# Order of TensorE's small products in the mixer head output: four full products, key transposes, then the 64-column products

## The reference, cut to what matters

```python
    scores = jnp.einsum('bhncd,bhnsd->bhncs', q_dec, k_inv)
    o_intra = jnp.einsum('bhncs,bhnse->bhnce', jnp.where(mask, scores, 0.0), vc)
    kv = jnp.einsum('bhnsd,bhnse->bhnde', k_end, vc)
    ...
    s_final, s_prev = lax.scan(step, s0.astype(f32), ...)
    o_inter = jnp.einsum('bhncd,bhnde->bhnce', q_dec, s_prev)
    o = (o_intra + o_inter).reshape(B, H, T, dv)
```

## Time and profile before

| | before |
|---|---|
| median of 3 runs | 1314.87 us |
| the profiled execution's span | 1315.8 us |
| PE busy | 97% of the span |
| PE weight loads (PEld) busy | 90% |
| DVE, ACT, POOL busy | 68%, 44%, 8% |
| mean granted TensorE clock | 0.990 |

### The profile page before, as it was taken

How to read it: one execution, slowest core, us unless ns; L and a number is a source line. 1 busy time by engine, 2 the same in 40 slices (tenths; PEclk the granted TensorE clock), 3 DMA queues, 4 the chain that set the end, 5 groups by cost and what they waited for, 6 DMA issues and landing times.

```text
span 1315.8 us, 24155 instructions
## 1 busy us (share of the span) xinstructions
PE 1277.5 (97%) x10293; PEld 1188.5 (90%) x10293; DVE 900.2 (68%) x1413; ACT 581.1 (44%) x908; POOL 110.0 (8%) x161
## 2 busy tenths in 40 slices
PE   6999999999999999999999999999999999999997
PEld 3899999999998778899998998998999898899997
DVE  4577755576464564678687786786888976767567
ACT  4533355644774444535413213223165664535431
POOL 0111111000001111000000001110000110000000
PEclk8999999999999999999999999999999999999999
DMA  9997896545244453222554456675435003555550
GB/s 354 382 317 238 264 250 168 144 151 182 75 160 157 165 172 133 88 91 80 175 158 148 144 177 192 188 239 161 133 100 194 29 1 102 188 160 193 183 170 33
DMA packets 170152, 218.39 MB, mean 166 GB/s; under 512 B 6158, under 2 KB 147861, under 8 KB 169910
## 3 DMA queue, kind: packets, MB, share of 16 engines
q1 hardware_dynamic: 140196, 148.11, 34.5%
q0 software_dynamic: 29152, 67.42, 17.0%
q10 hardware_dynamic: 698, 1.32, 0.3%
HBM read 215.70 MB, written 1.12 MB: 165 GB/s over the span
## 4 chain that ended last, share of the span: by engine, by line
PE 84%; DVE 8%; ACT 3%; issue 2%; DMA 2%; SPq 1%; POOL 0%; DVEq 0%; ACTq 0%
PE bank L1356 30%; PE bank L705 12%; PE bank L724 9%; PE bank L757 7%; PE bank L740 4%; DVE wlo L2154 2%; PE bank L1260 2%; PE bank L815 1%; PE bank L1334 1%; PE bank L906 1%; PE bank L1019 1%; PE bank L1434 1%; PE bank L1502 1%; DMA graw_b<-in_w_mod 1%; PE bank L1451 1%
## 5 line engine op out<-in xcount | busy, mean ns | idle before, releaser
L2154 DVE TENSOR_TENSOR wlo<-raw,whi 128x2048 fp32r<-128x2048 f32 x131 | 297.3, 2274 | 88.9 <-ACT whi L1545 88.5
L1545 ACT ACTIVATE whi<-raw 128x2048 fp32r<-128x2048 f32 x131 | 247.9, 1898 | 183.9 <-PE bank L1356 131.2
L1356 PE MATMUL bank<-a_lo,whi 128*128 128x256 f32 (+1 forms) x688 | 165.9, 312 | 0.0
L1356 PE MATMUL bank<-whi,m_hi 128*128 128x256 f32 x576 | 161.3, 280 | 1.2 <-DVE m_lo L2763 0.8
L1356 PE MATMUL bank<-whi,m_lo 128*128 128x256 f32 x576 | 160.6, 279 | 0.0
L1356 PE MATMUL bank<-wlo,m_hi 128*128 128x256 f32 x576 | 160.6, 279 | 0.0
L1356 PEld LDWEIGHTS bank<-a_lo,whi 128*128 128x128 f32 x688 | 112.3, 188 | 9.0
L1356 PEld LDWEIGHTS bank<-whi,m_hi 128*128 128x128 f32 x576 | 109.3, 190 | 1.9 <-DVE m_lo L2763 1.2
L1356 PEld LDWEIGHTS bank<-whi,m_lo 128*128 128x128 f32 x576 | 108.7, 189 | 0.0
L1356 PEld LDWEIGHTS bank<-wlo,m_hi 128*128 128x128 f32 x576 | 108.5, 188 | 0.1
L705 PE MATMUL bank<-h_hi,whi 128*128 128x256 f32 x336 | 95.0, 283 | 0.0
(11 more groups left out here) (451 smaller groups left out, 3420.2 us busy)
## 6 DMA issues: line engine op xcount, KB each, us to landing
raw<-in_mlp_w SPq DMA_DIRECT2D x64, 1024.0 KB, 5.2
raw<-in_w_in SPq DMA_DIRECT2D x32, 1024.0 KB, 8.2
graw_b<-in_w_mod POOLq DMA_DIRECT2D x64, 512.0 KB, 4.9
raw<-in_ev_w_in SPq DMA_DIRECT2D x12, 1024.0 KB, 5.1
pre<-in_w_ada SPq DMA_DIRECT2D x16, 512.0 KB, 9.6
graw_a<-in_w_mod POOLq DMA_DIRECT2D x16, 512.0 KB, 6.8
Y<-in_w_mod POOLq DMA_DIRECT2D x16, 512.0 KB, 4.3
raw<-in_od_w_qkv SPq DMA_DIRECT2D x6, 1024.0 KB, 5.0
```

The lines of the kernel that those rows point to most:

```text
L1356: mm = nc.tensor.matmul(o, x, y, start=(k == 0 and i == 0), stop=(k == KT - 1 and i == 2))
L1545: nc.scalar.activation(split_pair(u, kt * cols)[0], landing(u, kt * cols), ACT.Copy).then_inc(hi_done, 1)
L2154: nc.vector.tensor_tensor(split_pair(u, n)[1], landing(u, n), bf(whi[u % HI], n), ALU.subtract).then_inc(lo_done, 1)
```

## The change

`head_scores` is divided in `head_turn` (the four key transposes) and `head_products` (the eight score products), and `head_out` in `head_inside` (the four full products) and `head_across` (the eight 64-column products). For heads 0, 1, 2, 4, 5 and 6 a new function issues the four parts in the order inside, turn of the next head, across, products of the next head. For heads 3 and 7 it is inside, then across. The flag `start`, which makes a product overwrite the bank and not add to it, now stands at the first of the four full products alone. The wait for the states (`sp_done`) moves from ahead of the full products to ahead of the 64-column ones. No instruction is added or removed, and no other engine's order is changed.

```diff
+            def head_inside(hd):
 
                 h = hd % RH
                 pe.wait_ge(sc_done, hd + 1)
-                pe.wait_ge(sp_done, 2 * (hd + 1))
                 if hd:
                     pe.wait_ge(gy_done, hd)
                 for i in range(TILES):
                     nc.tensor.matmul(bank[3][:, i * P:(i + 1) * P], sc[hd % 2][:, i, :], vv[:, i, h * DV:(h + 1) * DV],
-                                     start=True, stop=False, skip_group_check=True)
+                                     start=(i == 0), stop=False, skip_group_check=True)
+
+            def head_across(hd):
+
+                h = hd % RH
+                pe.wait_ge(sp_done, 2 * (hd + 1))
+                for i in range(TILES):
                     for half in range(2):
                         c = 2 * i + half
                         mm = nc.tensor.matmul(bank[3][64 * half:64 * half + 64, i * P:(i + 1) * P], qd[:, h, c * CH:(c + 1) * CH],
                                               sp[hd % 2][:, c, :], start=False, stop=True, skip_group_check=True)
                 mm.then_inc(o_mm, 1)
+
+            def head_out(hd):
+
+                head_inside(hd)
+                head_across(hd)
+
+            def out_and_scores(hd):
+
+                head_inside(hd)
+                head_turn(hd + 1)
+                head_across(hd)
+                head_products(hd + 1)
...
-            head_out(0)
-            head_scores(1)
+            out_and_scores(0)
```

More of the change, by code:

```diff
@@ L1140, in decay_sums, with head_turn @@
                 mm.then_inc(bc_mm, 1)
-            def head_scores(hd):
+            def head_turn(hd):
                 h = hd % RH
@@ L1152, in head_scores, with head_products @@
                 mm.then_inc(kt_mm, 1)
+            def head_products(hd):
+                h = hd % RH
                 if hd:
@@ L1161, in head_scores @@
                 mm.then_inc(s_mm, 1)
+            def head_scores(hd):
+                head_turn(hd)
+                head_products(hd)
             def head_sums(hd):
@@ L1174, in head_sums @@
                 mm.then_inc(kv_mm, 1)
-            def head_out(hd):
+            def head_inside(hd):
                 h = hd % RH
                 pe.wait_ge(sc_done, hd + 1)
-                pe.wait_ge(sp_done, 2 * (hd + 1))
                 if hd:
@@ L1210, in _ @@
             mix_tile(E + 6, 1)
-            head_out(1)
-            head_scores(2)
+            out_and_scores(1)
             mix_tile(E + 7, 0)
@@ L1215, in _ @@
             mix_tile(E + 7, 1)
-            head_out(2)
-            head_scores(3)
+            out_and_scores(2)
             mix_tile(E + 8, 0)
@@ L1226, in _ @@
             mix_tile(E + 10, 0)
-            head_out(4)
-            head_scores(5)
+            out_and_scores(4)
             mix_tile(E + 10, 1)
@@ L1231, in _ @@
             mix_tile(E + 11, 0)
-            head_out(5)
-            head_scores(6)
+            out_and_scores(5)
             mix_tile(E + 11, 1)
@@ L1267, in _ @@
             gy_turn(0)
-            head_out(6)
-            head_scores(7)
+            out_and_scores(6)
             gy_turn(1)
```

## The result

The changed kernel takes 1304.17 us, the median of 4 runs (1302.50 to 1304.79), against 1314.9 us of the kernel before beside it (1314.62 to 1315.61). The ratio is 0.9902, with a 95% interval of 0.9888 to 0.9917. It is 10.7 us faster; 10.5 were forecast, and the forecast range was 1302.2 to 1307.5.

The account below looks back on a forecast made before the run. PE was taken as the bound, losing time at head outputs where the array's form changes. Woven heads 7.2, head 3 1.05, head 7 2.1 and head 6 0.1 sum to 10.5 us: 1314.87 to 1304.4 us, range 1302.2 to 1307.5.

Parts of the forecast that it names:

- Woven heads: Outputs of heads 0, 1, 2, 4, 5, 6: 3.62 us each against 4.83, together 7.2 us gained.
- free or 0.24 us dearer: Unseen change from 64 columns to 64 rows in woven heads: free adds 0.9 us gain, dearer takes 1.4 off.
- Head 3: Only the inside order changes: 3.15 us becomes 2.09, 1.05 gained; the wait for DVE's L2173 behind stays 0.67 us.
- Head 7: Full products run within PE's wait for the states: 2.1 us gained; PE reaches L1296 with 0.5 us to spare.
- Head 6: Its output also passes a short wait for the states: 0.1 us gained.
- The way to the end: Behind the mixer PE's waits stay the same and DVE is not behind, so the whole gain arrives.
- Does it reach the end?: Part on whether the mixer's gain survives: all 10.5 us should, give or take 1.2; profiled span 1305.3 us.
- the waits for the `graw_b` DMA: Mixer waits of PE held fixed, because the DMA is issued when PE has used the tile.
- the clock: Half-clock stretches near 1092, 1122 and 1153 us could fall elsewhere, shifting the sum by 1.2 us either way.
- The stall is not bank 3's: Rival at head outputs: once-only time belongs to adding onto written bank 3; 4.8 us less gain, 1309; chance 0.03.
- openly paid: Rival in 64-column runs: weight loads not hidden, 0.13 us more a step, 8 us in all, 1312.6; chance 0.02.
- Nothing waits for the transposes: Rival: transposes ahead of 64-column products wait for qk_done or kir_done; 7.5 us lost, 1322; chance 0.03.

Follow-up runs that it names:

- the early wait: Changed kernel with the wait for the states (sp_done) put back in front of the full products; 1306.26 us, ratio to before 0.9907.
- alternate turns: Changed kernel, but in six heads each 64-column pair is followed by one transpose of the next head; ratio to before 0.9964.
- grouped and not woven: Changed kernel with the next head's transposes put back behind the 64-column products; 1307.22 us, ratio to before 0.9914.
- the quarters: Changed kernel with the two quarters (L815) of heads 0 to 5 moved to just ahead of the 64-column products; 1303.18 us, ratio to before 0.9897.
- giving up the neighbourhood: Changed kernel issuing four 64-column products of the lower array half, then four of the upper, not alternating halves; 1309.07 us, ratio to before 0.9940.
- the last version: Changed kernel with the quarters (L815) moved ahead of the 64-column products, except at head 3; 1302.47 us, ratio to before 0.9876.

## Why the prediction was right, and which terms were not

The step that carried it was to read a price from the places where a form of the array follows itself and from those where it changes.

- **Woven heads.** Worked out 3.62 us, measured 3.64: 1.19 us times six, 7.1 us. The change that no row of before showed, from 64 columns to 64 rows, costs what the others do (405.94 + 1.02 to 406.96). Neither bound of it, free or 0.24 us dearer, was needed. By the Trainium skill (TensorEngine Tiling (Array Packing), section Key Properties) a change of tiling mode drains the engine and a change of tile does not. The trace agrees on both: 0.15 us for each of seven added changes of form, and no idle time for the change of half.
- **Head 3.** 3.15 us became 2.11, 1.04 gained against 1.05. The wait for DVE behind it stayed (0.47 us on PE's row against 0.67).
- **Head 7.** 2.15 us against 2.1, half of it by the place of the wait, as the early wait shows. In the view of the chain PE reached L1316 (L1296 before) at 547.69, 6.7 us after the output, and did not wait there: DVE had ended L2508 at 547.12, 0.6 us earlier where 0.5 were worked out.
- **Head 6.** The step from the transposes to the output is 0.15 us shorter where 0.1 was worked out, and the early wait takes it back. It is too small to be told from chance in the times.
- **The way to the end.** It is open, as forecast: the same waits of the same length after 541 us, and a distance of 10.2 to 11.2 us from there to the attention.

The mechanism held, and so did the sum for the mixer. **The step that failed** is in the part "Does it reach the end?", where what lies around the head outputs was taken as fixed but for 1.2 us. The profiled execution should have had a span of 1305.3 us. It had 1302.7, and two more executions of the same kernel, on other chips, had 1305.4 and 1300.2. Three terms were mis-sized.

The first is the waits for the `graw_b` DMA, which I held fixed, since they hang on PE's own release. They are not: the step of head 5 in which they stand takes 19.46, 18.41 and 18.22 us in the three executions. That is as much as a head's gain.

The second is the clock. I took the number of half-clock stretches as fixed and let one fall elsewhere, 1.2 us either way. The number is what changes, four before and two, three and one after, and the spans of the changed kernel alone lie 5.2 us apart while their mixers differ by 0.85. I had also counted three stretches, from 1092 on. There is a fourth in the same execution, at 358 us, in front of the mixer:

```profile
355.00:365.00 10.00, 10.00 (x54) 8.09 (x53) 0.61 (x2) 9.89 (x17) 0.00 (x0) 0.83 0.34 105
```

It ran 54 products where the changed kernel ran 63. The third is the pace of the big products, which the sum put at nothing: steps of 0.114 or 0.118 us, 1.5 us in the last MLP and 0.5 in the mixer.

The stretch at 358, the one at 1092 and the pace of the last MLP make up most of the difference between the 13.1 us of the spans and what the mixer gave. The medians differ by 10.7. That this is within 0.2 us of the 10.5 is in part luck: on the two other chips where both kernels ran they differ by 13.0 and 15.5 us, with a mixer that gave 10.8 each time. No run shows where the rest of that comes from, since the kernel before has no trace there.

One reading of the rows was loose: not each group ends with an idle time of 0.17 us, only those behind a pair and behind the transposes do. The sums were made from the starts of the weight loads and do not use it.

The rivals fell. The stall is not bank 3's (alternate turns, and the stall in front of the score products in the version that is grouped and not woven). Weight loads of one row group are not openly paid: 16 loads of 137 ns in 0.85 us, and here the rule of the Trainium skill (TensorE: Matmul & The Clock Gate, The mechanism) that they overlap running matmuls only when the row groups differ does not hold. Nothing waits for the transposes.

## What to carry to other kernels

Look for the idle time of the weight loads that "issue" ends. Here it repeated within a group that waited for nobody, at places where the array changes its form, and ordering the products by form took it away. Read the steps between starts, since a change can cost its 0.15 to 0.2 us and show no idle time. "issue" can also hide a wait for another engine, as the 1.64 us in front of head 7 did. Put work that needs less (here the full products) ahead of the wait, and what needs the late input behind it. Before work is moved back, follow who reads its result, and what that engine does next in its fixed order: what the quarters gave at the other heads, they lost at head 3, where ACT had to read their product before it took the squares that DVE waited for.

## What the runs showed that I had not expected

The big products have two paces at a granted clock of 1.00. Their weight loads come every 0.113 to 0.114 us in some stretches and every 0.118 in others, and one stretch of one kernel has either from one execution to the next: the 48 products ahead of the sums of head 7 take 0.118 us each in the first execution of the changed kernel and 0.114 in the second and third. No run tells what decides it.

Two 64-column products of different halves run side by side even when four products of one half stand in front of the other half's: 7 weight loads begin within 0.38 us in the overlap, against one every 0.109 us around it. The cost of giving up the neighbourhood was 0.49 us a head and not 0.87.

The change from the 32-column quarters to a full product leaves 0.41 us of idle weight loads, but the change from those same quarters to the 64-column products also has 0.41 us, and that from transposes to the quarters only 0.17. So the 0.41 go with leaving the quarters and not with what comes next. The starts of the single records tell what most of it is: the last four weight loads of the quarters start at 405.45 and their products only at 405.66, one step later, and the first 64-column product starts at 405.99. Between products it is 0.33 us, where the quarters among themselves have a step of 0.22. So the change adds 0.11 us, and the rest of the idle time is weights that were loaded ahead.

```profile
404.99 0.59 PEld L815 LDWEIGHTS bank<-graw_b,cwide 128*32 128x32 f32 x16 [0.17 <-issue]
405.99 0.85 PEld L1202 LDWEIGHTS bank<-sp,qd 128*64 128x64 f32 x16 [0.41 <-issue]
```

These two rows are of the last version. From the sums of head 0 to those of head 1 it was 18.41 us in one execution with the moved quarters and 18.22 in the other, against 18.41 in the changed kernel. The pace of the big products is the reason: their 94 steps between these points take 11.06 us in the first, 10.88 in the other and 10.87 in the changed kernel.
